# Second layer's normalised input turned by one transposing DMA for each tile of 128 tokens, in place of sixteen identity matmuls and two evictions

## The reference

```python
def reference(x, ...):
    for layer in range(DEPTH):
        i = layer // 2
        if layer % 2 == 0:
            h = rms_norm(x, ln_pre_even[i])
            o = even_mixer(h, w_in_even[i], pool_w[i], pool_scale[i], w_out_even[i])
            x = x + rms_norm(o, ln_post_even[i])
        else:
            h = rms_norm(x, ln_pre_odd[i])
            o = odd_mixer(h, w_in_odd[i], sconv_w[i], dconv_w[i], dconv_b[i], cnorm_g[i], cnorm_b[i], w_out_odd[i])
            x = x + rms_norm(o, ln_post_odd[i])
    return x
```

## Time and profile before

| | us |
|---|---|
| three runs | 2297.71, 2519.85, 2673.37 (median 2519.85) |
| profiled execution, its own time | 2297.7 |
| span of the slowest core (6) in it | 2296.3 |
| spans of the eight cores | 2288.4 to 2296.3 |
| mean granted TensorE clock, by core | 0.993 to 0.995 |
| PE busy, share of the span | 96% |
| DVE, ACT, POOL busy | 45%, 31%, 27% |

### The profile page before, as it was taken

The page is one execution under the profiler, slowest core; times in us unless marked ns, Lnnn a source line. Parts: engine busy times, 40 slices in busy tenths (PEclk is TensorE's granted clock), DMA queues, the critical chain, the costliest instruction groups (busy, mean ns, idle before and its releaser), DMA issues.

```text
span 2296.3 us, 39547 instructions; the slowest of 8 cores (2288.4 to 2296.3 us)
## 1 busy us (share of the span) xinstructions
PE 2198.8 (96%) x13498; PEld 1170.5 (51%) x13740; DVE 1039.8 (45%) x1270; ACT 706.2 (31%) x1378; POOL 624.2 (27%) x616
## 2 busy tenths in 40 slices
PE   5899999999999899999999999999899999999997
PEld 3444566667777444444444555544344444444443
DVE  5500278777777657734443232326632222332222
ACT  3511155555555431134442221243200000002221
POOL 0000055555555421133332333420000000003333
PEclk9999999999999999999999999999999999999999
DMA  9542022222112332944444424436522222583444
GB/s 234 138 65 28 1 30 29 29 30 29 14 18 39 47 56 37 140 136 147 147 148 84 73 44 68 65 45 111 112 37 37 38 37 37 74 131 127 147 158 154
DMA packets 124212, 179.12 MB, mean 78 GB/s; under 512 B 22769, under 2 KB 104945, under 8 KB 113393
## 3 DMA queue, kind: packets, MB, share of 16 engines
q0 software_dynamic: 99344, 71.83, 23.9%
q1 hardware_dynamic: 24674, 104.74, 14.3%
HBM read 198.04 MB, written 33.55 MB: 101 GB/s over the span
## 4 chain that ended last, share of the span: by engine, by line
PE 86%; DMA 5%; issue 2%; DVE 2%; POOL 2%; ACT 1%; SPq 1%; DVEq 0%; POOLq 0%; ACTq 0%
PE ps L267 42%; PE ps L778 17%; PE ps L519 8%; PE ps L537 5%; PE ps L917 3%; PE ps L613 3%; PE ps L601 2%; PE ps L578 2%; DMA yp<-Rc 1%; PE ps L455 1%; SPq L145 1%; POOL xr L800 1%; DMA xr<-x 1%; DMA w1s<-w1s 1%; DMA wg<-w0g 1%
## 5 line engine op out<-in xcount | busy, mean ns | idle before, releaser
L267 PE MATMUL ps<-R,w1s 128*128 128x512 bf16 x2008 | 441.9, 380 | 13.9 <-DMA w1s<-w1s 11.8
L593 POOL TENSOR_TENSOR At<-Cr 128x512 bf16<-128x512 f32 (+1 forms) x320 | 289.9, 912 | 359.2 <-DVE Cr L589 311.2
L267 PEld LDWEIGHTS ps<-R,w1s 128*128 128x128 bf16 x2048 | 200.7, 98 | 255.1 <-issue 14.7
L267 PE MATMUL ps<-R,wg 128*128 128x512 bf16 x1311 | 295.4, 382 | 1.9 <-issue 0.2
L800 POOL TENSOR_TENSOR xr<-xr,tmp 128x512 f32<-128x512 f32 x128 | 162.2, 1267 | 336.3 <-DVE tmp L797 182.3
L519 PE MATMUL ps<-R,wh 128*128 128x512 bf16 x982 | 244.6, 379 | 2.2
L589 DVE TENSOR_TENSOR_SCAN Cr<-ps,Cr,zer 128x512 f32<-128x512 f32 (+1 forms) x192 | 207.8, 1082 | 47.1 <-ACT ps L584 33.1
L584 ACT ACTIVATE ps<-ps 128x512 f32<-128x512 f32 (+1 forms) x320 | 166.0, 519 | 202.4 <-PE ps L578 107.3
L267 PE MATMUL ps<-R,w1c 128*128 128x512 bf16 x1000 | 222.0, 379 | 3.1 <-DVE tmp L797 1.8
L267 PEld LDWEIGHTS ps<-R,wg 128*128 128x128 bf16 x1344 | 131.3, 99 | 156.3 <-issue 6.4
L604 ACT ACTIVATE ATt<-ps 128x512 bf16<-128x512 f32 (+1 forms) x320 | 169.4, 529 | 6.9 <-PE ps L601 6.2
(11 more groups left out here) (130 smaller groups left out, 2339.0 us busy)
## 6 DMA issues: line engine op xcount, KB each, us to landing
xr<-x SPq DMA_DIRECT2D x16, 1024.0 KB, 8.0
x1s<-xr SPq DMA_DIRECT2D x16, 1024.0 KB, 5.4
w1s<-w1s POOLq DMA_DIRECT2D x8, 2048.0 KB, 16.1
xr<-x1s SPq DMA_DIRECT2D x16, 1024.0 KB, 6.9
out<-xr SPq DMA_DIRECT2D x16, 1024.0 KB, 4.8
wh<-w0h POOLq DMA_DIRECT2D x8, 1536.0 KB, 16.0
xt<-x SPq DMA_DIRECT2D x8, 1024.0 KB, 14.0
xq<-x SPq DMA_DIRECT2D x8, 1024.0 KB, 17.8
```

What stands on the lines that cost most here:

```text
L267: fns = [lambda dc=dc: T.matmul(banks[b][:, 0:n], lhsT=w[:, dc, c0:c0 + 128], rhs=rhs[:, dc, lo:lo + n], start=(dc == 0), stop=(dc == 15)) ...
L593: k.op(pool, lambda: G.tensor_tensor(out=a[:, 0:n], in0=C[:, 512 * c:512 * c + n], in1=C[:, 512 * c + 1:512 * c + 1 + n], op=SUB), reads=[ ...
```

## The change

`k.dma` gets a flag that makes the DMA a transposing one. `next_norm` no longer returns the sixteen transposes and two evictions to be run later. It issues at once, from SP, one DMA that reads `xn` (128 tokens x 2048 channels, bf16, 0.5 MB) and writes it turned into the tile's columns of `R1` (128 channels x 16 chunks x 128 tokens). It waits for `xn` to be written, and for the previous DMA on its channel (two channels, tiles even and odd). `out_phase` itself, with its order of loads and stores, is as before; `pend_n` now holds functions that do nothing.

```diff
-    def dma(self, eng, pairs, chan, reads=(), writes=()):
+    def dma(self, eng, pairs, chan, reads=(), writes=(), tp=False):
         self._deps(eng, reads, writes)
         if chan.cnt:
             eng.wait(Tok(chan.sem, chan.sid, chan.cnt))
         for out, in_ in pairs:
             chan.cnt += 16
-            eng.h.dma_start(out=out, in_=in_).then_inc(chan.sem, 16)
+            if tp:
+                eng.h.dma_start(out=out, in_=in_, transpose=True).then_inc(chan.sem, 16)
+            else:
+                eng.h.dma_start(out=out, in_=in_).then_inc(chan.sem, 16)
...
+        trc = [k.chan(), k.chan()]
+
         def next_norm(n, i, xr, xrb):
             xnt, xnb = xn1[n % 2]
             b = Buf()
...
             k.op(dve, lambda: V.scalar_tensor_tensor(out=xnt[:], in0=xr[:], scalar=rs, in1=gpre1[:], op0=MUL, op1=MUL),
                  reads=[xrb, b, gpre1b], writes=[xnb])
-            return lambda: tr_evac(xnt, xnb, R1, i, h1b, 6, 7)
+            k.dma(sp, [(R1[:, :, i * 128:(i + 1) * 128], xnt[:])], trc[n % 2], reads=[xnb], writes=h1b[i], tp=True)
+            return lambda: None
```

## The result

The changed kernel is **slower: ratio 1.0317, 95% interval 1.0303 to 1.0331**. Its five executions took 2368.95 to 2573.77 us, median 2372.01; the kernel before took 2297.71 and 2298.62 us in its two quickest of five. In the others (2519.85, 2673.37 and 2715.7, and here 2538.03 and 2573.77) the cores of one die or of both ran at a lower granted clock whatever the kernel, and the ratio leaves them out. The loss is about 73 us of 2298; 113 was forecast.

What follows compares the result with a forecast made beforehand. PE was taken as the bound, with the `xr` loop 0.2 us behind; 25 us for the stage, -8 for the tail and 16 X at X = 6.0 gave +113 on 2297.7, 2411 us, range 2350 to 2555.

Steps and rivals of the forecast that it cites:

- `xr` loop: Layer 0's `out_phase`: load of `xr`, adds on POOL, store, next load; 14.5 us a tile, capping any gain at 3 us.
- The order of SP's queue: Next load stands behind norm and transposing DMA: issued 5.73 us after the store, period 16.3 us plus X against 14.64.
- X: What one 0.5 MB transposing DMA adds per tile, on SP and the DMA engines together; taken as 6.0 us.
- I take 6.0: Choice of X in us, from 16 `Z<-dt` DMAs of 64 KB holding SP 11.91 us for 1 MB.
- my upper bound: X if small packets cost 88 ns each: 128 per engine, 11.3 us, sum +198.
- The tail: Last store to `glu(0, 0)`: 14.3 + X us against 22.4 before, so a change of X - 8.1.
- Sum: Stage and tail together: 25 - 8 + 16 X = 17 + 16 X us added.
- Copy speed: Rival: the transposing DMA in the stage costs like a copy, X 1.6, sum +43, 2341 us; chance 0.11.
- Block by block: Rival: each transposing DMA is worked off as sixteen 128x128 blocks, X 20 us, 2635 us; chance 0.12.
- Clock: Rival: PE, idling in each tile, stays at the lower clock throughout, 27.6 us a tile, 2491 us; chance 0.04.
- The low end of the range: Lower edge of the forecast time, 2350 us, said to take in copy speed's 2341 with 3 us below it.

Runs made afterwards that it cites:

- the wait: Kernel before, with SP made to wait for `xn` between a tile's store and the next load, no transposing DMA: ratio 1.012, median 2324.88 us.
- the halves: Changed kernel with each transposing DMA cut into two of 8 chunks, same bytes: ratio 1.0355.
- Early load: Next tile's load issued ahead of this tile's store: changed kernel 0.9955, kernel before 1.0, changed kernel with last tile turned by PE 0.995.

## Why the prediction was right in its mechanism and wrong in its size

- **What bounded the stage.** Right that PE and the `xr` loop were nearly equal. Wrong by how much the second capped a gain: I allowed 3 us, the transposing DMA behind the next load gives 8 in the stage (218.7 to 210.4). The load's 8.1 us from issue to first add was no floor: with the transposes off PE it is 7.1 us in several tiles, a loop of 13.4 us and not 14.5, with slower tiles between. And six of the eight cores show 218.7 or 218.8 us, PE's own pace; core 6, from which I read 14.64 a tile and a chain through the load, was the one that strayed.
- **The order of SP's queue.** Right: 5.73 us from store to load with an ordinary issue was forecast, 5.25 with no issue at all was measured, and the load alone lands in 4.9 us where 4.8 was taken. A period of 16.3 + X against 16.35 measured for the wait. The transfer from one row (the `out<-xr` stores) to another held.
- **The step that failed: "I take 6.0".** X is 2.9 us. That is the whole of the miss in the stage: 15 x 3.1 = 46 us. I priced one DMA of 0.5 MB by eight issues of 64 KB DMAs, that is by what SP needs for many instructions; the halves show that the price does not go by issues. The packets were right in number (252 bytes, 2080 a tile) but my upper bound took 88 ns for each from a queue of other packets. Counted the same way, the queue that held nothing but transposing DMAs (issued by ACT) spent 2.1% of 16 engines x 2392.5 us on 33,280 packets, 24 ns each: 128 of them are 3.1 us, close to X.
- **The tail.** I forecast X + 2 us to land and X - 8 for the tail, -5 at X = 3. It is +1.4 by the medians. The last DMA lands in 10.1 us, not in 5, beside the `w1c` load, which I had not placed there; without that load the tail is 19.7, which is 4.6 under before, as the sum had it. PE waits 4.31 us for that DMA, and then begins `glu(0, 0)` partly at the lower clock (granted 0.72 from 1296 to 1302 us): 62 matmuls in 15.23 us, where 62 at full clock took 13.97 in the kernel before. The wait and the clock are 5.6 of the 6.0 us between 25.7 and 19.7.

```profile
1296.94 15.23 PE L270 MATMUL ps<-R,w1c 128*128 128x512 bf16 x62 [4.31 <-DMA R<-xn]
```

- **Sum.** With X = 2.9 the same sum gives 17 + 46 = 63 us; the tail's 6 to 7 us bring it to 70, measured 73.
- **Rivals.** *Copy speed* is what happened in kind, if the copy is one in 256-byte runs: the Trainium skill's sentence ("Advanced Engine Details and Errata", section "X-Bar Transpose (TRN2)") that transposing DMAs are as fast as regular ones holds here, 19.29 us a tile for both, 4.3 us to landing for both. It does not hold against a copy in 4 KB runs (3.0 us). My price for it, 1.6, was the 4 KB price, measured as 1.3. *Block by block* is refuted: sixteen blocks land in 4.3 us together. *Clock*: see the last section; it costs nothing in the stage. Whether the 1.86 us of the earlier trace rows were the clock stays open, as the granted clock reads 1.00 there.
- **The low end of the range.** It is written as 2350 and then said to lie 3 us under 2341, which is 2338. The two do not fit, and 2350 leaves out the copy-speed price.
- **The base of the number.** 2411 us was set on the execution of 2297.7. Read against the median given for the kernel before, 2519.85, it looks like a gain, which none of its steps forecasts; and the measured ratio put on that median would be 2600 us, above my range. The median of the changed kernel, 2372.01, lies within it. So beside X this step failed too: a number on one quick execution was given without saying what it means on the median. The forecast should have been written as a ratio, 2411 / 2297.7 = 1.049, against 1.0317 measured.

## What to carry to other kernels

A DMA that waits for a result holds every DMA behind it in its queue. Before such a DMA is added, look at what stands next: here the next tile's load, which the adds, the freeing of the banks and so PE wait for. Put the wait behind the loads, or issue the loads a tile earlier; moving the DMA to another engine's queue only moves the question to what stands behind it there. And moving work off a full engine pays only by the distance to the next loop: early loads alone gave nothing, transposing DMAs alone lost 3%, the two together gained half a per cent.

## What the runs showed of the hardware

- One transposing DMA of 128 x 2048 bf16 lands in 4.3 us and holds SP for 2.07 (changed kernel, core 3; the other cores' medians are 1.89 to 2.11). With it behind the load, where the DMA engines were busier (share 0.64 against 0.45), the issue took 2.7 to 4.5 us for the first fifteen on core 2. A plain DMA in the place of the changed kernel's is issued in 0.47 (4 KB runs) or 0.61 us (256 bytes).
- A load behind a transposing DMA is issued in 0.74 to 0.99 us in place of 0.33 (changed kernel, core 3), and behind the copy in 256-byte runs in 0.91 to 1.29 (core 7).
- PE's granted clock does fall after a gap, and the rows of the changed kernel show it directly. In the tile behind the one shown PE idles nearly 4 us. Over the next 3.5 us the mean granted clock is 0.55, so it ran nearly all of them at the lower of its two levels (1.2 and 2.4 GHz), and then it is back (same columns as above):

```profile
1092.00:1096.50 4.50, 0.59 (x3) 0.10 (x1) 3.37 (x5) 2.65 (x9) 0.00 (x0) 0.97 0.29 72
1096.50:1100.00 3.50, 3.46 (x9) 1.26 (x10) 0.56 (x1) 0.00 (x0) 0.00 (x0) 0.55 1.04 237
1100.00:1104.00 4.00, 4.00 (x20) 1.86 (x19) 0.49 (x1) 0.00 (x0) 1.66 (x2) 1.00 0.33 139
```

It did so after this gap of 3.95 us and not after the one of 3.27 a tile earlier (granted 1.00 from 1070.18 to 1089.06); yet it did after the one of 3.10 in the tail shown under **Early load**. In a stage that waits for a load this is hidden: the tiles from 1070.18 and from 1089.06 both take 18.88 us, the second at a mean granted clock of 0.91. In the tail it is not: 1.7 us there.
